# Gate rows of chunked attention loaded by spreading DMAs instead of built on TensorE, and key products kept for the other direction

## What is computed

```
w = b_last[..., None] - b + li
kv_chunk = jnp.einsum('bhcsk,bhcsv->bhckv', kc * ew[..., None], vc)
...
C_new = a[..., None, None] * C + g[..., None, None] * kv_c
...
D = b[..., :, None] - b[..., None, :] + li[..., None, :]
D = jnp.where(causal, D, -jnp.inf)
inter = ms[..., None] + b
m_t = jnp.maximum(inter, jnp.max(D, axis=-1))
wts = jnp.exp(D - m_t[..., None])
sc = jnp.exp(inter - m_t)
qk = jnp.einsum('bhctk,bhcsk->bhcts', qc, kc) * wts
num = jnp.einsum('bhcts,bhcsv->bhctv', qk, vc) + sc[..., None] * jnp.einsum('bhctk,bhckv->bhctv', qc, Cs)
```

## Time and profile before

| | us |
|---|---|
| median of 3 runs | 1868.33 |
| lowest and highest run | 1868.33, 1871.32 |
| the profiled execution, whole | 1868.85 |
| its span, first to last instruction | 1866.5 |

### The profile page before, as it was taken

The page is one execution under the profiler, slowest core; times in us unless marked ns, Lnnn a source line. Parts: engine busy times, 40 slices in busy tenths (PEclk is TensorE's granted clock), DMA queues, the critical chain, the costliest instruction groups (busy, mean ns, idle before and its releaser), DMA issues.

```text
span 1866.5 us, 27369 instructions
## 1 busy us (share of the span) xinstructions
PE 1832.8 (98%) x10922; PEld 1714.4 (92%) x10922; DVE 1080.2 (58%) x2279; ACT 711.8 (38%) x1220; POOL 214.0 (11%) x232
## 2 busy tenths in 40 slices
PE   7999999999999999999999999999999999999997
PEld 2999999999999999999998899999999999888886
DVE  2663545545545544346364569777777777656563
ACT  3633321234232324254143454444444444443432
POOL 2000000000000010011000042222222221001111
PEclk9999999999999999999999999999999999999999
DMA  9133223323323353148232231333233234868682
GB/s 350 36 87 94 70 75 94 90 75 119 106 47 118 108 131 121 64 169 279 69 114 90 85 106 67 108 107 98 96 99 101 97 100 163 295 226 286 227 282 93
DMA packets 202563, 239.96 MB, mean 129 GB/s; under 512 B 9944, under 2 KB 162548, under 8 KB 202436
## 3 DMA queue, kind: packets, MB, share of 16 engines
q1 hardware_dynamic: 185204, 174.88, 29.8%
q0 software_dynamic: 12736, 45.56, 7.3%
q10 hardware_dynamic: 4496, 17.77, 2.3%
HBM read 180.50 MB, written 57.68 MB: 128 GB/s over the span
## 4 chain that ended last, share of the span: by engine, by line
PE 91%; DVE 4%; ACT 2%; DMA 1%; issue 1%; SPq 0%; ACTq 0%; POOL 0%; DVEq 0%; POOLq 0%
PE ps L1203 22%; PE ps L1231 14%; PE ps L886 13%; PE ps L888 13%; PE ps L887 13%; PE ps L1141 5%; PE ps L1022 2%; PE ps L1025 2%; PE ps L1024 1%; PE ps L928 1%; PE ps L1001 1%; DVE H_lo L1791 1%; DMA adaw<-in_w_ada_dram 1%; PE ps L913 1%; ACT Wt L1462 1%
## 5 line engine op out<-in xcount | busy, mean ns | idle before, releaser
L886 PE MATMUL ps<-H_hi,ring_hi 128*128 128x384 f32 x1416 | 491.3, 347 | 6.3 <-DVE H_lo L1791 4.4
L888 PE MATMUL ps<-H_hi,ring_lo 128*128 128x384 f32 x1416 | 474.6, 335 | 0.0
L887 PE MATMUL ps<-H_lo,ring_hi 128*128 128x384 f32 x1416 | 474.4, 335 | 0.0
L886 PEld LDWEIGHTS ps<-H_hi,ring_hi 128*128 128x128 f32 x1416 | 266.4, 188 | 10.3 <-DVE H_lo L1791 5.5
L887 PEld LDWEIGHTS ps<-H_lo,ring_hi 128*128 128x128 f32 x1416 | 266.6, 188 | 1.1
L888 PEld LDWEIGHTS ps<-H_hi,ring_lo 128*128 128x128 f32 x1416 | 266.1, 188 | 0.0
L1939 DVE SCALAR_TENSOR_TENSOR Cst<-Cst,Et,ps 128x257 f32<-128x257 f32 x64 | 30.9, 484 | 222.1 <-PE ps L1025 222.1
L1203 PE MATMUL ps<-T_lo,up_hi 128*128 128x288 f32 x608 | 130.3, 296 | 0.0
L1203 PE MATMUL ps<-T_hi,up_lo 128*128 128x288 f32 x608 | 130.2, 296 | 0.0
L1203 PE MATMUL ps<-T_hi,up_hi 128*128 128x288 f32 x608 | 130.2, 296 | 0.0
L1791 DVE TENSOR_TENSOR down_lo<-down_raw,down_hi 128x1024 fp32r<-128x1024 f32 x66 | 80.7, 1223 | 76.8 <-ACT f_hi L1699 76.8
(11 more groups left out here) (278 smaller groups left out, 3298.9 us busy)
## 6 DMA issues: line engine op xcount, KB each, us to landing
down_raw<-in_w_down_dram SPq DMA_DIRECT2D x66, 512.0 KB, 3.8
raw<-in_w_in_dram SPq DMA_DIRECT2D x44, 512.0 KB, 3.9
up_raw<-in_w_up_dram SPq DMA_DIRECT2D x38, 512.0 KB, 5.2
raw<-in_w_ada_dram SPq DMA_DIRECT2D x32, 512.0 KB, 4.9
f_raw<-z_gate SPq DMA_DIRECT2D x66, 192.0 KB, 3.6
v_raw<-z_value SPq DMA_DIRECT2D x66, 192.0 KB, 4.0
z_gate<-mid_g SPq DMA_DIRECT2D x38, 288.0 KB, 4.1
z_value<-mid_v SPq DMA_DIRECT2D x38, 288.0 KB, 4.7
```

What stands on the lines that cost most here:

```text
L886: pe.matmul(out, whi, xhi, start=first, stop=False)
L887: pe.matmul(out, whi, xlo, start=False, stop=False)
L888: return pe.matmul(out, wlo, xhi, start=False, stop=last)
```

## The change

The rows of `g` and of exp(`y`) are written to DRAM once (`z_gates`), the first by POOL, the second by ACT, during unit 6. For each step SP issues two DMAs (`gates_load`), one for each direction; each reads one pair of rows, 1 KB, and writes it to all 128 partitions of one of four slots of `GE`. DVE adds the key number and the mask in place (`gate_arguments`, two instructions), for the step after the one it is in and ahead of the present step's `attention_weights`. ACT takes the exponential in place, also one step ahead. The scores part of PE keeps key-query products and key transposes alone, at positions 0 to 4; ACT copies those of positions 1 to 4 to `SC`, where positions 5 to 8 read them. At position 0 one product and one transpose serve both directions. The norm's square root and scalings move one step later. At the end, POOL waits one load earlier for the end of the attention.

```diff
+    GE = place("GE", [P, GSLOTS, 2, 2, P])
-    Wt = place("Wt", [P, 2, P])
-    Et = place("Et", [P, 2, P])
-    sel = place("sel", [P, 8, P], F32R)
+    SC = place("SC", [P, SEEN, 4, P])
...
+            def gates_load(x):
+
+                if x == 0:
+                    sp.wait_ge(g_rows_stored, 32)
+                    sp.wait_ge(e_rows_stored, 32)
+                if x >= GSLOTS:
+                    sp.wait_ge(att_state, 2 * (x - GSLOTS + 1))
+                h, i = x // NT, x % NT
+                for d, cx in enumerate(step_tiles(i)):
+                    sp.dma_start(GE[:, x % GSLOTS, d, :, :], z_gates[d, h, cx].partition_broadcast(P)).then_inc(gates_in[x % GSLOTS], 16)
...
                 sp.dma_start(dst, src).then_inc(landed[n % RS], 16)
+                if it[0] == "unit" and 0 <= it[1] - SEG - 2 < NT * NH:
+                    gates_load(it[1] - SEG - 2)
...
-                if e:
-
-                    pe.wait_ge(att_weights, e)
-                for d, cx in ((0, cf), (1, cb)):
-                    tok = slice(cx * P, (cx + 1) * P)
-                    j = d * NH + h
-                    o = d * P
-                    pe.matmul(ps[:, 3, o:o + P], idbf[:, :], maskbf[:, d, :], start=True, stop=False)
-                    pe.matmul(ps[:, 3, o:o + P], sel[:, j, :], GS[:, tok], start=False, stop=True)
-                    pe.matmul(ps[:, 3, 256 + o:256 + o + P], sel[:, j, :], YS[:, tok], start=True, stop=True)
-                    pe.matmul(ps[:, 4, o:o + P], kT[v][:, tok], qT[v][:, tok], start=True, stop=True)
-                    mm = pe.transpose(ps[:, 4, 256 + o:256 + o + P], kT[v][:, tok], ident[:, :])
+                if i >= 2:
+                    pe.wait_ge(att_weights, NT * h + i - 1)
+                    pe.wait_ge(att_cached, SEEN * h + i - 2)
+                for d, cx in enumerate(step_tiles(i)):
+                    if i or d == 0:
+                        tok = slice(cx * P, (cx + 1) * P)
+                        pe.matmul(ps[:, bank, d * P:(d + 1) * P], kT[v][:, tok], qT[v][:, tok], start=True, stop=True)
+                        mm = pe.transpose(ps[:, bank, (2 + d) * P:(3 + d) * P], kT[v][:, tok], ident[:, :])
                 mm.then_inc(att_scores, 1)
...
+                def exps():
+
+                    e = seg + 1
+                    if 0 <= e < NT * NH:
+                        act.wait_ge(gate_args, e + 1)
+                        w = GE[:, e % GSLOTS, :, 0, :]
+                        act.activation(w, w, ACT.Exp).then_inc(att_exps, 1)
+                    if m - 1 in NORM_AT:
+                        hm_roots(NORM_AT[m - 1])
...
+            def gate_arguments(e):
+
+                h, i = e // NT, e % NT
+                dve.wait_ge(gates_in[e % GSLOTS], 32 * (e // GSLOTS + 1))
+                for d, cx in enumerate(step_tiles(i)):
+                    row = GE[:, e % GSLOTS, d, 0, :]
+                    ins = dve.scalar_tensor_tensor(out=row, in0=row, scalar=a_tok[:, cx, d, h:h + 1], in1=mask[:, d, :],
+                                                   op0=ALU.add, op1=ALU.add)
+                ins.then_inc(gate_args, 1)
...
+                if 0 <= seg + 1 < NT * NH:
+                    gate_arguments(seg + 1)
                 if seg >= 0:
-                    h, i = seg // 9, seg % 9
+                    h, i = seg // NT, seg % NT
                     attention_weights(h, i)
+                    if m - 1 in NORM_AT:
+                        head_scale(NORM_AT[m - 1])
                     attention_outputs(h, i, 0)
                     attention_outputs(h, i, 1)
```

More of the change, by code:

```diff
@@ L73, in shape_constants @@
     out[:, H_ID:H_ID + P] = np.eye(P)
-    for d in range(2):
-        for h in range(NH):
-            r = 32 * d + h
-            for row in (r, 64 + r):
-                out[row, H_SEL + (d * NH + h) * P:H_SEL + (d * NH + h + 1) * P] = 1.0
     s, t = np.arange(P)[:, None], np.arange(P)[None, :]
@@ L123, in build @@
     LS = 5
+    GSLOTS = 4
+    SEEN = (NT - 1) // 2
+    HALF = SEEN + 1
     ADA0 = 16
@@ L260, in build @@
     qs = place("qs", [P, 2, P])
-    sel = place("sel", [P, 8, P], F32R)
+    SC = place("SC", [P, SEEN, 4, P])
     ada_part = place("ada_part", [P, 2, P])
     ones = place("ones", [P, 1])
-    idbf = place("idbf", [P, P], BF16)
-    maskbf = place("maskbf", [P, 2, P], BF16)
+    mask = place("mask", [P, 2, P], BF16)
     assert base[0] <= nc.sbuf_usable_end, (base[0], nc.sbuf_usable_end)
@@ L538, in down_slot_free, with step_tiles, gate_row_tiles @@
             eng.wait_ge(down_used, n - DR - r + 1)
+    def step_tiles(i):
+        return (0, 0) if i == 0 else (i, NT - i)
+    def gate_row_tiles(r, d):
+        return Gt[r][32 * d:32 * d + NH, :].rearrange("p (t s) -> p t s", s=P)
     def evac_main(act, q0, dst, scale, after_first):
@@ L763, in _ @@
             pool.dma_start(nm[1].rearrange("(r c) -> r c", c=1), Gt[4][32:36, 0:1]).then_inc(new_m_stored, 16)
+            for d in range(2):
+                pool.dma_start(z_gates[d, :, :, 0, :], gate_row_tiles(5, d)).then_inc(g_rows_stored, 16)
             for h in range(NH):
@@ L1510, in _ @@
                     put((kind, idx), q0 + 3)
+                if seg >= 0 and 1 <= seg % NT < HALF:
+                    act.wait_ge(att_weights, seg + 1)
+                    act.activation(SC[:, seg % NT - 1, :, :], ps[:, 3 + seg % NT % 2, :].rearrange("p (a b) -> p a b", b=P),
+                                   ACT.Copy).then_inc(att_cached, 1)
                 for group, step in pool_steps(m):
@@ L1861, in _ @@
             norm_split(0, tsc, 4, 2, direct=False)
[L1863 to L1866 removed]
             def gates():
+                dve.wait_ge(consts_in, 16)
+                dve.tensor_copy(mask[:, :, :], mask32[:, :, :])
                 dve.memset(Gt[3][0:GR, :], 0.0)
@@ L1909, in attention_weights @@
             def attention_weights(h, i):
-                e = h * 9 + i
-                tiles = (0, 0) if i == 0 else (i, NT - i)
-                v = h % 2
+                e = h * NT + i
+                v, bank = h % 2, 3 + i % 2
+                W, E = GE[:, e % GSLOTS, :, 0, :], GE[:, e % GSLOTS, :, 1, :]
                 dve.wait_ge(att_exps, e + 1)
-                dve.tensor_tensor(Pt[:, :, :].rearrange("p a b -> p (a b)"), ps[:, 4, 0:256],
-                                  Wt[:, :, :].rearrange("p a b -> p (a b)"), ALU.mult)
+                if i < HALF:
+                    dve.wait_ge(att_scores, HALF * h + i + 1)
+                    part = lambda n: ps[:, bank, n * P:(n + 1) * P]
+                else:
+                    dve.wait_ge(att_cached, SEEN * (h + 1))
+                    part = lambda n: SC[:, NT - 1 - i, n, :]
@@ L1917, in attention_weights @@
+                if 1 <= i < HALF:
+                    dve.tensor_tensor(Pt[:, :, :], ps[:, bank, 0:2 * P].rearrange("p (a b) -> p a b", b=P), W, ALU.mult)
+                else:
+                    for d in range(2):
+                        dve.tensor_tensor(Pt[:, d, :], part(0 if i == 0 else 1 - d), W[:, d, :], ALU.mult)
                 if i:
-                    for d, cx in enumerate(tiles):
-                        dve.tensor_tensor(qs[:, d, :], qT[v][:, cx * P:(cx + 1) * P], Et[:, d, :], ALU.mult)
+                    for d, cx in enumerate(step_tiles(i)):
+                        dve.tensor_tensor(qs[:, d, :], qT[v][:, cx * P:(cx + 1) * P], E[:, d, :], ALU.mult)
@@ L1920, in attention_weights @@
                 for d in range(2):
                     last = (1 - d) * (P - 1)
-                    ins = dve.tensor_scalar(k_weighted[:, d, :], ps[:, 4, 256 + d * P:256 + (d + 1) * P], Wt[:, d, last:last + 1], None,
-                                            ALU.mult)
+                    n = 2 if i == 0 else 2 + d if i < HALF else 3 - d
+                    ins = dve.tensor_scalar(k_weighted[:, d, :], part(n), W[:, d, last:last + 1], None, ALU.mult)
                 ins.then_inc(att_weights, 1)
@@ L1990, in gate_branch_b, with head_scale @@
                     dve.tensor_tensor(mixF[:, d, tok], ps[:, 3 + b, 0:BW], tiles[:, wb, tok], ALU.mult).then_inc(evac1, 1)
+            def head_scale(h):
+                dve.wait_ge(head_squares, NT * (h + 1))
+                dve.tensor_scalar(hstat[:, 0, :], hstat[:, 0, :], 1.0 / DV, EPS, ALU.mult, ALU.add).then_inc(head_roots, 1)
+                dve.wait_ge(head_roots, 2 * h + 2)
+                link(dve.reciprocal(hstat[:, 0, :], hstat[:, 1, :]))
+                for t in range(NT):
+                    ins = dve.tensor_scalar(hm[h % 2][:, t, :], hm[h % 2][:, t, :], hstat[:, 0, t:t + 1], None, ALU.mult)
+                ins.then_inc(hscaled, 1)
             gates()
```

106 lines of the change are left out of this document (41 added, 65 removed).

## The result

| | median, us | lowest and highest run | ratio to before, 95% interval |
|---|---|---|---|
| before | 1868.88 | 1868.33, 1871.32 | |
| after | 1965.74 | 1960.82, 1970.75 | 1.0516 (1.0487 to 1.0545) |

Both rows are medians of four runs. The change makes the kernel 5.2% slower, 97 us. The forecast was 1914 us, with a range up to 1960. The direction was right; the loss is twice the one forecast, and the time lies 6 us outside the range. The profiled execution took 1970.75 us, its span is 1968.8.

A forecast was written before the change was run, and what follows sets the result against it. PE, busy 98%, was taken to bound the kernel. From 1868.85 us, +46.7 for 24 waiting steps and -14.7 for the other steps and the norm gave 1900.9; 13.6 for clock falls made 1914 us, range 1880 to 1960.

The forecast's parts named there:

- The 24 steps: Attention steps 0 to 9, 12 to 18 and 21 to 27, where gate load and use fall together: +46.7 us.
- the 15.5 us of a step at positions 5 to 8: PE work in an attention step without turn work: 16.88 us before, less 1.35.
- the gain of 39.5 us without waits: Attention, if nothing else moved: 34.9 us of work taken from PE and 4.6 us of norm waits.
- the 1.35 us: Cost on PE of step 5's scores part, all of which positions 5 to 8 lose.
- the norm's order: Square roots and scalings moved behind the weights on ACT and DVE: three PE waits go, 4.6 us.
- X: Time from SP's issue of the weights to the landing of both gate loads: 4.7 us, between 3.8 and 5.5.
- the clock's falls: PE at half clock behind the eight longest stalls, 1.7 us each: 13.6 us; with all 24, 1942 us in total.
- 7.13: Microseconds from the end of the weights to the second state update, forecast without a clock fall.
- The loop of 14.64 + X: Waiting attention step, from last state update to the next step's: 19.34 us, against 16.88 before.
- The whole gain: Rival: no attention step waits, 1829 us; needs a load time below 1.6 us; chance 0.03.
- the overtaking rows: Rival: gate rows land ahead of the weights, after 3.0 us as for a load alone: 1860 us; chance 0.05.
- the third: Rival: 128 reads of one address served one after the other, adding 2.3 us or more: 1956 to 1997 us; chance 0.10.

The follow-up runs named there:

- the early load: Changed kernel with the gate rows issued one unit earlier, so that they land a step before use: 1828.74 us, ratio 0.9783 to the kernel before.
- the other order on DVE: Changed kernel with `gate_arguments` of the next step behind `attention_weights` of the present step on DVE, loads unchanged: 1834.38 us, ratio 0.9817 to the kernel before.
- half the filling: Changed kernel with 10 (positions 0 to 4) or 14 (5 to 8) unread identity products ahead of PE's wait in the 24 steps: 1926.4 us, ratio 1.0307.

## Why the prediction was right or wrong

**Right: what bounds, and the order.** The issue tied to the modulation products, and `gate_arguments` ahead of the weights, were read from trace and code, and the early load, or the other order on DVE, takes the loss away. The 24 steps came out, and the 15.5 us of a step at positions 5 to 8 (with the early load), and the gain of 39.5 us without waits (40.3 measured). Steps 32 to 35 take 15.1 us (869.97 to 885.08) and not the 15.5 named; before they took 16.47, not 16.88, so the 1.35 us taken from them is right. The total of 39.5 holds better than its parts: the kept products brought 10.2 us for 12.2, and the norm's order more than its 4.6.

Two terms of the sum failed: X, put at 4.7 us, was 5.7 on average, and the clock's falls, put at 13.6 us, cost 46.3.

**Wrong, first: X.** Named 4.7 us from a slope of bytes; it is 5.2 in step 4 and 5.3 in most. Two parts of it were too small. Behind the weights the two gate loads take SP 1.05 us to issue (above), not 2 x 0.37 as the loads of the earlier trace rows; that is 0.3 us. This is not the spreading: ahead of the weights the same two take 0.81, and behind them it is 1.05 from 128 addresses too. The rest is the landing, 4.1 us from its own issue. It is slow for two reasons, of which each alone is nearly enough (4.2 and 3.8 us in the table): the weights in front, and 128 reads of one address. The prediction had the second only as a rival that would begin at X = 7. It was not a rival; it was at work in a smaller size. In five steps (1, 3, 15, 23, 24) the load took up to 4 us more behind the weights. These steps are near normal where it went ahead, but for step 1; what else ran there was not settled. Over the 24 steps X is 1.03 us too small on average, 24.7 us in the sum.

The Trainium skill, DMA: Bandwidth & Descriptors, section Queues, rings and completion order, has each engine take a ring's descriptors in order. With 128 addresses the landing rises from 2.2 to 3.8 us when the weights go first, and the weights' own from 4.0 to 4.3 when they go second, which agrees.

**Wrong, second: the clock, the larger part.** I put a fall behind the eight longest stalls, at 1.7 us each, since the norm's waits of up to 1.8 us showed none. It fell behind 23 of 24. The size of one fall was right (8.7 - 7.13 = 1.6 us), its number was not, and in seven steps it lasted 6.8 us and cost 2.8. What sets the two kinds apart in the trace is when the fall begins: in the seven, 0.6 to 1.2 us before PE starts again, in the single ones at most 0.5 before, and up to 1.1 us after. The stalls of the seven are 3.3 to 4.4 us long, those of the single ones 2.4 to 5.0, so the length alone does not tell. Why it begins when it does stays open. The cost was 46.3 us in place of 13.6. The same sentence gave 1942 for all 24. A longer X made the stalls longer, but it does not explain the falls: ahead of the weights, with X about as named, the clock still fell behind 19 of 24, and the kernel was 22 us above the forecast, of which X explains 4.7. So the error in the clock stands by itself.

The loop of 14.64 + X held within 0.2 us where the clock did not fall: in step 14 the products' end to `gate_arguments` is 5.85, which gives 14.64 + 5.82 = 20.46, and the step took 20.61. With half the filling it holds as well in all steps at positions 1 to 8 whose clock stayed up.

**The range.** 1961 stood in the text as the forecast's upper end, X at 4.7 + 0.8 and all falls. The measured time is that end and 5 us more. It had the number of falls about right. What the range left out were the five steps in which the load came 1 to 4 us later still, so that the mean X was 5.7 and not 5.5, and falls of double length.

**The rivals.** The whole gain and the overtaking rows fell for this kernel; the first is what happens when the rows come a step earlier. The X below 1.6 us that was named for it is right at positions 1 to 4 alone; at 5 to 8 a step of 15.5 us leaves 15.5 - 14.64 = 0.9. The time of the third (1956 to 1997) came true, but by luck: the slow read of one address was there, at well under the 2.3 us that it asked for, and over half of the miss was the clock.

**The norm.** I took its 4.6 us of waits as its whole worth. On the faster kernel it is 16.7: the same order meets an earlier PE and a longer DVE, and the clock falls.

## What to carry to other kernels

Before a load is put ahead of work that another engine waits for, find the event to which its issue is tied and subtract: here one index (the trigger one unit earlier) or two lines on VectorE turn 5% of loss into 2% of gain. When TensorE, busy 98%, is made to wait a few microseconds in every step, price the clock behind the wait beside the wait itself: here 46 us of half clock came with 90 us of waiting, and stalls of 2 us could bring it. And a small row that is spread over 128 partitions is not small: it is 128 reads of one address, and wants lead time. Copies of it might serve too, which no run tried with the gate values.

## What the runs showed of the hardware

- Many reads of one row in DRAM are slow. Two loads of 128 KB, each 128 reads of 1 KB, with nothing ahead of them, land after 2.2 us (median of both) from 128 rows, after 4.2 to 4.3 from one row for each, and after 5.3 from one row for both. Whether the address or its part of DRAM counts was not separated. I had expected nothing or far more.
- This and a longer load ahead in the queue do not add: 4.2 us, 3.8 us, and 4.1 with both.
- Two gate loads take SyncE 1.05 us to issue behind the 512 KB of weights and 0.81 ahead of them, from one address or from 128.
- TensorE's granted clock went to 0.50 behind 23 of 24 stalls of 2.4 to 7.5 us in the changed kernel, for 3.4 us or 6.8 (10.2 once, from within the longest). One stall of 3.5 us saw none. With the gate loads ahead of the weights it fell behind 19 of 24, the shortest of 1.8 us, and 5 of 1.8 to 2.6 us saw none. So the length of a stall alone did not decide. Work that nobody reads in the stall left 2 falls in the 24 steps and was worth 39 us.
- An identity product of 128 x 128 in float32 is two instructions and takes 0.22 us.
